# Weight loads of the state-space stage one tile sooner, the first blocks loaded in halves, the last blocks computed in column halves

## What is computed

```python
for i in range(DEPTH):
    hn = rmsnorm(h, g_mix[i])
    mix = mla_mixer(hn, ...) if i == 0 else s5_mixer(hn, ...)
    h = h + mix
    h = h + conv_ffn(rmsnorm(h, g_ffn[i]), ...)
return rmsnorm(h, g_final)
# s5_mixer
u = h @ w_in                                   # 64 groups of 16 channels
x_t = a * x_{t-1} + B u_t ; y = Re(C x) + D * u  # 64 complex states a group
y = gelu(y); val, gate = split(y @ w_glu); return val * sigmoid(gate)
```

## Time and profile before

| | |
|---|---|
| median of 3 runs | 1143.05 us (1139.31 to 1145.65) |
| the profiled execution's own time | 1146.58 us |
| its span in the profile | 1144.8 us |
| mean granted PE clock | 0.987 of full speed |

### The profile page before, as it was taken

How to read it: one execution, slowest core, us unless ns; L and a number is a source line. 1 busy time by engine, 2 the same in 40 slices (tenths; PEclk the granted TensorE clock), 3 DMA queues, 4 the chain that set the end, 5 groups by cost and what they waited for, 6 DMA issues and landing times.

```text
span 1144.8 us, 14849 instructions
## 1 busy us (share of the span) xinstructions
PE 1116.7 (98%) x5678; PEld 919.5 (80%) x5678; DVE 788.6 (69%) x1202; ACT 476.4 (42%) x721; POOL 57.9 (5%) x154
## 2 busy tenths in 40 slices
PE   8999899999999999999998999999999999999996
PEld 5787778888888888888887887888888888888885
DVE  6657857688787788978855885546765477635665
ACT  5556554455423543345451324334442244423442
POOL 3072004000000000000000000000000000000000
PEclk8999999999999999999998999999999999999998
DMA  6311103233343332433376663332333223232222
GB/s 210 102 59 52 37 20 111 78 114 126 106 130 111 116 123 92 148 111 120 89 260 202 175 186 93 94 109 75 109 95 108 93 92 95 90 111 92 93 78 87
DMA packets 62966, 125.68 MB, mean 110 GB/s; under 512 B 21808, under 2 KB 32560, under 8 KB 62896
## 3 DMA queue, kind: packets, MB, share of 16 engines
q1 hardware_dynamic: 61744, 120.54, 33.4%
q0 software_dynamic: 1152, 4.19, 1.1%
HBM read 110.04 MB, written 14.68 MB: 109 GB/s over the span
## 4 chain that ended last, share of the span: by engine, by line
PE 87%; DVE 5%; DMA 3%; DVEq 2%; ACT 1%; issue 1%; SPq 0%; ACTq 0%
PE bank L1507 27%; PE bank L1509 27%; PE bank L1508 27%; DVE MX L1057 1%; PE bank L1850 1%; DVE P L1065 1%; DVEq L1056 1%; PE bank L1799 1%; PE bank L1842 1%; DMA RAW<-in_w_wa 1%; ACT WH L505 1%; DMA RAW<-in_w_glu 1%; DVE WL L862 1%; DVE X L1289 1%; DMA ud_scratch<-UB 0%
## 5 line engine op out<-in xcount | busy, mean ns | idle before, releaser
L505 ACT ACTIVATE WH<-RAW 128x1024 fp32r<-128x1024 f32 (+1 forms) x184 | 190.0, 1034 | 392.2 <-PE bank L1509 352.6
L1507 PE MATMUL bank<-GH,WH 128*128 128x512 f32 x816 | 323.1, 396 | 3.2 <-DVE GL L920 3.2
L1508 PE MATMUL bank<-GL,WH 128*128 128x512 f32 x816 | 319.6, 392 | 0.0
L1509 PE MATMUL bank<-GH,WL 128*128 128x512 f32 x816 | 319.5, 392 | 0.0
L862 DVE TENSOR_TENSOR WL<-RAW,WH 128x1024 fp32r<-128x1024 f32 (+1 forms) x184 | 219.1, 1191 | 54.4 <-ACT WH L505 53.7
L1507 PE MATMUL bank<-AH,WH 128*128 128x512 f32 x596 | 235.2, 395 | 1.9 <-DVE WL L862 1.1
L1509 PE MATMUL bank<-AH,WL 128*128 128x512 f32 x596 | 232.2, 390 | 0.0
L1508 PE MATMUL bank<-AL,WH 128*128 128x512 f32 x596 | 232.0, 389 | 0.0
L1507 PEld LDWEIGHTS bank<-GH,WH 128*128 128x128 f32 x816 | 154.5, 189 | 36.7 <-DVE GL L920 4.1
L1509 PEld LDWEIGHTS bank<-GH,WL 128*128 128x128 f32 x816 | 154.5, 189 | 32.6
L1508 PEld LDWEIGHTS bank<-GL,WH 128*128 128x128 f32 x816 | 154.6, 189 | 32.4 <-issue 0.7
(11 more groups left out here) (270 smaller groups left out, 930.9 us busy)
## 6 DMA issues: line engine op xcount, KB each, us to landing
RAW<-in_w_up SPq DMA_DIRECT2D x88, 512.0 KB, 3.5
RAW<-in_w_dn SPq DMA_DIRECT2D x32, 512.0 KB, 3.5
RAW<-in_w_glu SPq DMA_DIRECT2D x16, 512.0 KB, 3.5
RAW<-in_w_dn SPq DMA_DIRECT2D x16, 384.0 KB, 3.0
RAW<-in_w_wo SPq DMA_DIRECT2D x8, 512.0 KB, 3.5
od_scratch<-OO SPq DMA_DIRECT2D x8, 512.0 KB, 3.7
kd_scratch<-KT SPq DMA_DIRECT2D x8, 512.0 KB, 4.9
O<-od_scratch POOLq DMA_DIRECT2D x8, 512.0 KB, 4.5
```

The costliest lines, as they stand in the source:

```text
L505: act_(WH[b % RH][:, :n], RAW[b % RW][:, :n], ACT.Copy).then_inc(s_hi, 1)
L1507: mm(out, wh, hi_[:, k, :], start=start, stop=False)
L1508: mm(out, wh, lo_[:, k, :], start=False, stop=False)
L1509: return mm(out, wl, hi_[:, k, :], start=False, stop=stop)
```

## The change

Three places are changed.

**Start.** Blocks 0 and 1 are loaded, split and consumed by halves of four units: first halves between the first x tiles, second halves behind x tile 3. One matmul of zeros fewer; PE takes two units of each block first, not three. Small tables go in another order, and on ACT and DVE blocks 2 and 3 are split between the squares at other points; the exponential of `ld` stands behind the squares.

**State-space stage.** In step t SP loads block win+5+t, where it loaded win+4+t, so each load stands one step ahead. TM4 and O2 of tile 4 come one step later. On DVE the low part of y tile 4 goes behind the states of the last tile.

**End.** The last three blocks are computed for columns 0 to 255 first, then for columns 256 to 511, with the sums, roots and spreading of the first half between the matmuls of the second. ACT multiplies tiles 0 to 6 by the gain beforehand, so DVE scales by the factor alone, in four instructions a half (3, 2, 2 and 1 tiles), each followed by its DMA.

```diff
-LAGS_AT = {1: 4, 3: 3, 4: 5, 6: 7}
+LAGS_AT = {2: 4, 3: 3, 4: 5, 6: 7}
...
+            def load_half(b, h):
+                sp.dma_start(RAW[b][:, HALF_W[h]], d["w_wa"][b][:, HALF_W[h]]).then_inc((s_rawh if h == 0 else s_raw)[b], 16)
...
+            load_half(0, 0)
+            x_in(0)
+            sp.dma_start(GAIN[:], d["gain"]).then_inc(s_par, 16)
+            x_in(1)
+            load_half(1, 0)
+            x_in(2)
+            x_in(3)
+            load_half(0, 1)
+            load_half(1, 1)
+            for k in range(4, KD):
+                x_in(k)
             load(2)
+            for n in ("lr", "li", "ld"):
+                sp.dma_start(small[n][:], d[n]).then_inc(s_sml, 16)
+            load(3)
...
                 if t >= 3:
                     y_out(t - 3)
-                if t >= 1:
-                    load(FIRST["win"] + 4 + t)
+                load(FIRST["win"] + 5 + t)
                 if t in LAGS_AT:
                     lags_in(LAGS_AT[t])
...
-            for k in range(4):
+            for k in range(2):
                 add_square("x", k, first=(k == 0))
             lo(2)
-            for k in range(4, KD):
+            for k in range(2, 6):
                 add_square("x", k)
             lo(3)
+            for k in range(6, KD):
+                add_square("x", k)
...
+            def final_squares(h):
+                for i, j in enumerate(LAST3):
+                    act.wait_ge(s_xh, 3 * h + i + 1)
...
+                    act_(SQ[j % 2][:, HALF[h]], X[:, j, HALF[h]], ACT.Square).then_inc(s_sqh, 1)
+                    if j < KD - 1:
+                        act_(X[:, j, HALF[h]], X[:, j, HALF[h]], ACT.Identity, scale=gain("final", j)).then_inc(s_xg, 1)
...
                     states(t - 2)
-                if t >= 4:
+                if t == NJ + 1:
+                    y_lo(t - 5)
+                if t >= 4 and t != NJ:
                     y_lo(t - 4)
...
+            final_add(KD - 1, 0)
             final_factor(0)
-            final_scale(0, range(0, 3))
+            final_add(KD - 3, 1)
+            final_scale(0, PARTS[:1])
+            final_sum(KD - 3, 1)
+            final_scale(0, PARTS[1:2])
+            final_add(KD - 2, 1)
...
-            pool.wait_ge(s_ur[1], 16)
+            pool.wait_ge(s_ur[2], 16)
             fetch(4)
...
-            for _ in range(5):
+            for _ in range(4):
                 mm(bank[3][:], ONES[:], WARM[:], start=True, stop=True)
...
+            def last_half(j, h, ks):
...
+                for k in ks:
+                    wh, wl = (w[b % RH][:, k * P:(k + 1) * P] for w in (WH, WL))
+                    out = bank[LAST[j, h]][:, HALF[h]]
+                    mm(out, wh, AH[:, k, HALF[h]], start=(k == 0), stop=False)
+                    mm(out, wh, AL[:, k, HALF[h]], start=False, stop=False)
+                    m = mm(out, wl, AH[:, k, HALF[h]], start=False, stop=(k == THIRDS[2][1] - 1))
...
+            for j in LAST3:
+                last_half(j, 0, range(6))
+            last_half(KD - 3, 1, range(4))
+            final_sums(0)
+            last_half(KD - 3, 1, range(4, 6))
+            last_half(KD - 2, 1, range(2))
+            final_spread(0)
+            last_half(KD - 2, 1, range(2, 6))
+            last_half(KD - 1, 1, range(6))
+            final_sums(1)
+            final_spread(1)
```

More of the change, by code:

```diff
@@ L698, in next_tile @@
                 square(X[:, j, :], SQ[j % 2], key, j)
+                if kind == "final":
+                    act_(X[:, j, :], X[:, j, :], ACT.Identity, scale=gain(kind, j)).then_inc(s_xg, 1)
             for j, b in enumerate(span("wo")):
@@ L850, in _ @@
             ffn(1, ("n_glu", "n_dn12", "final"))
-            final_std()
+            act_(STD[:], STD[:], ACT.Sqrt)
+            for h in range(2):
+                final_squares(h)
+                final_std(h)
         @block.vector
@@ L1258, in ffn @@
                     for j, b in enumerate(span(f"dn{l}{t}")):
+                        last = t == 2 and j == KD - 1
+                        if l == 1 and t == 2 and j in LAST3:
+                            continue
                         dve.wait_ge(s_mm, nth(b))
[L1260 to L1263 removed]
                         add_x(b, j)
@@ L1597, in spread @@
                 m.then_inc(s_sel, 1)
-            some(0, range(0, 3))
-            some(1, range(0, 3))
-            for k in range(3, KD):
+            some(0, range(0, 2))
+            some(1, range(0, 2))
+            for k in range(2, KD):
                 some(0, (k,))
@@ L1814, in ffn, with final_sums, final_spread @@
                             matrices(MAT_AT[b])
-                        whole(b, n, AH, AL)
+                        if b < NBLOCKS - 3:
+                            whole(b, n, AH, AL)
+            def last_half(j, h, ks):
+                b = NBLOCKS - KD + j
+                if 0 in ks and h == 0:
+                    ready(b)
+                for k in ks:
[4 more added lines that the diff above has]
+                    m = mm(out, wl, AH[:, k, HALF[h]], start=False, stop=(k == THIRDS[2][1] - 1))
+                if THIRDS[2][1] - 1 in ks:
+                    m.then_inc(s_lh, 1)
+            def final_sums(h):
+                pe.wait_ge(s_ssh, 2 * h + 2)
+                pe.wait_ge(s_sqh, 3 * h + 3)
+                for t in range(2):
+                    cols = slice((2 * h + t) * P, (2 * h + t + 1) * P)
+                    mm(bank[2 + 2 * h][:, t:t + 1], SS[:, cols], ONES[:, 0:1], start=True, stop=False)
+                    m = mm(bank[2 + 2 * h][:, t:t + 1], SQ[1][:, cols], ONES[:, 0:1], start=False, stop=True)
+                m.then_inc(s_mh, 1)
+            def final_spread(h):
+                pe.wait_ge(s_rch, h + 1)
+                for t in range(2 * h, 2 * h + 2):
+                    m = spread_column(bank[3 + 2 * h], t)
+                m.then_inc(s_bch, 1)
             ffn(0, "n_wo", TILE0["n_wo"])
```

160 lines of the change are left out of this document (86 added, 74 removed).

## The result

The changed kernel takes 1133.32 us (median of 5 runs, 1130.49 to 1135.14), the kernel before 1141.43 on the same chip (median of 5, 1139.31 to 1145.65). The ratio is 0.9921, with a 95% interval of 0.9904 to 0.9938: 9 us faster by the ratio (8.1 by the medians), where 14.2 were forecast. The median stands above the forecast's own range (1124.5 to 1132.5) and inside the wide one (1124 to 1135.5). The profiled execution took 1132.29 us.

A forecast was written before the change was run, and what follows sets the result against it. PE's queue of matmuls, busy 98% of the span, was taken as the bound. Start -6.0, state-space stage -7.5 and end -0.7 make -14.2, from 1143.05 to 1129 us; own range 1124.5 to 1132.5, wide range 1124 to 1135.5.

The forecast's parts named there:

- Start, -6.0: First 30 us: halved blocks bring PE's sums of x from 29.62 to 23.4; 6.0 us saved, bounds -2.5 to -7.0.
- the order of issue: Start: DMAs landing strictly as issued would bring old x tile 1 at about 5.9; the trace said 8.13.
- State-space stage, -7.5: Earlier load of win+5 shrinks PE's XI wait and keeps the clock up: 7.5 us saved, bounds -2.6 to -8.8.
- The delay of U, +1.0: State-space stage: the moved load collides with tile 0's read of U, making PE wait 1.0 us more (0 to 1.5).
- The other two waits for XI (0.8 us): State-space stage: PE's two shorter waits for XI have the same cause as the long one and go too, 0.8 us.
- The 3.89 us for the clock: State-space stage: low clock behind the long XI wait, 11.49 us against 7.60 to the next inputs; goes with the wait.
- End, -0.7: Last three blocks in column halves, half the scaling hidden: span ends 0.7 us sooner, bounds +1.5 to -2.5.
- outputs at 340 GB/s to the end: End: expected sign in the trace, the output DMAs running at that rate until the span ends.
- The start keeps a wait that costs the clock: Rival: x tile 1 and block 1 share the DMA rate; start gives only -2.5, total 1132.4; chance 0.15.
- rival of half-width matmuls bound by weight loads: End: 0.162 us per load sets the step, 108 matmuls take 17.5 us; end +4.5, total 1134.1; chance 0.06.
- rival of SP's queue: State-space stage: loads waiting on a later low part delay each of eight tiles; slower than before, 1149; chance 0.03.
- rival of a slow stretch that stays: State-space stage: tile 0's U comes later behind 0.5 MB of weights; stage only -2.6, total 1133.8; chance 0.10.

The follow-up runs named there:

- end alone: Only the edits of the end, on the kernel before: 1141.40 us (11 runs), ratio 0.9996.
- stage alone: Only the edits of the state-space stage, on the kernel before: 1134.33 us (5 runs), ratio 0.9919.
- without start: The whole change with its edits at the start undone: 1130.64 us (4 runs), ratio 0.9905.
- old start, states first: The whole change with its start undone and, on DVE, tile 0's states ahead of the low part of block win+5: 1130.32 us (6 runs), ratio 0.9908.
- one load: The kernel before with only the load of block win+5 moved, from step 1 to step 0: 1136.67 us (5 runs), ratio 0.9957.
- one load, low part last: The kernel before with block win+5 loaded in step 0 and y tile 4's low part behind the last tile's states: 1138.62 us (12 runs), ratio 0.9966.
- start alone: Only the edits of the start, on the kernel before: 1140.94 us (12 runs), ratio 0.9991.
- whole again: The changed kernel unedited, timed and traced a second time: 1132.30 us (4 runs), ratio 0.9907.
- whole third: The changed kernel unedited, timed and traced a third time: 1132.77 us (5 runs), ratio 0.9920.
- without end: The whole change with its edits at the end undone: 1134.36 us (6 runs), ratio 0.9929.
- states first: The whole change with, on DVE, tile 0's states ahead of the low part of block win+5: 1130.72 us (4 runs), ratio 0.9900.

## Why the prediction was right in its range and wrong in its terms

All 13 traces, cut at four marks of PE's timeline: the sums of x; from the first KH,QH matmul of attention to the inputs of tile 0 (between these two marks lie 71.2 or 71.3 us in every trace); from there to the XR matmuls of the last tile; from there to the end of the span.

| trace | start | sums of x | attention to inputs | stage | rest |
|---|---|---|---|---|---|
| before | old | 29.62 | 503.58 | 81.88 | 458.46 |
| end alone | old | 26.39 | 501.93 | 82.96 | 457.20 |
| stage alone | old | 24.59 | 503.22 | 75.15 | 458.32 |
| without start | old | 24.37 | 501.90 | 73.27 | 457.21 |
| old start, states first | old | 24.49 | 501.87 | 72.84 | 457.46 |
| one load | old | 24.46 | 501.91 | 77.71 | 458.26 |
| one load, low part last | old | 24.28 | 502.00 | 75.71 | 458.38 |
| start alone | new | 22.51 | 503.49 | 82.07 | 458.72 |
| after | new | 22.67 | 502.47 | 76.56 | 457.48 |
| whole again | new | 23.22 | 503.41 | 76.73 | 458.02 |
| whole third | new | 23.25 | 503.67 | 73.27 | 457.99 |
| without end | new | 23.39 | 503.70 | 77.17 | 458.71 |
| states first | new | 23.09 | 504.06 | 72.83 | 457.51 |

**Start, -6.0: mis-sized, the term that failed.** The new start was forecast well: the sums at 23.4, measured 23.02 as the mean of six. Wrong was what it was held against. The step took x tile 1 at 8.13 and block 1 at 9.94 as the kernel's own and gave the reason that "later transfers took part of the rate"; then it counted the 2.32 us wait and 15 matmuls at the low clock as what the change could take away. Six other traces of the same instructions have the sums at 24.28 to 26.39; in five of them the clock from 10 to 20 us is 1.00 although PE waits up to 1.47 us for GL. The 8.13 that the prediction held against the order of issue was that run's own as well: in the other six ACT takes x tile 1 at 6.1 to 6.54, where that order gave 5.9. Over seven old and six new traces the start gives 25.46 - 23.02 = 2.4 us. And 1.1 of it is gone before the first inputs (502.34 on average with the old start, 503.47 with the new). Part of that is systematic: PE's last wait for P in attention is 0.91 or 0.92 us in all seven traces with the old start and 1.26 or 1.27 in all six with the new, behind a gap on DVE that nothing in the profile explains. PE and DVE of after:

```profile
141.59 0.55 PE L1787 MATMUL bank<-IDENT,P 128*128 128x128 f32 x3 [1.27 <-DVE P L1108]
```

```profile
140.27 0.69 DVE L1100 TENSOR_REDUCE MX<-bank 128x1 f32<-128x512 f32 x1 [0.42 <-issue]
```

The rest is a drop of the clock between 100 and 130 us, in five of six new traces and two of seven old ones. The whole third and the old start with the states first, same stretch:

```profile
105.00:110.00 5.00, 5.00 (x22) 3.73 (x21) 3.22 (x14) 2.70 (x10) 0.00 (x0) 0.70 0.02 5
```

```profile
105.00:110.00 5.00, 4.52 (x26) 3.73 (x27) 4.21 (x16) 3.78 (x12) 0.00 (x0) 1.00 0.02 5
```

Both had just waited 1.61 us for P at the same matmul. Whether the new start makes this drop likelier, or seven and six traces fell so, was not settled. Net the start is worth 1.3 us by the traces, and only 0.4 without the trace of before (24.76 and 502.14 on the old side); timed alone 0.8 (up to 2.6, or nothing), and in the whole it did not show at all. Why x tile 1 and block 1 landed so late in the one trace is open.

**State-space stage, -7.5: right in size, by two errors of opposite sign.** The stage's mean is 82.30 in the three traces with the old loads and 75.36 in the six with the new ones: -6.9. By its steps: the landing of 4.8 us was exact, and XI came 0.51 us late instead of 0.3. The delay of U, +1.0, was not there: PE waits 0.25 us for the first U (0.38 before), and from its read to its inputs pass 3.03 us with the load right behind (3.15 before), so 0.5 MB issued 0.4 us later took nothing from it. (The sum also takes off the 0.3 us that, by the prediction's own words, the 1.0 would hide.) The other two waits for XI (0.8 us) went, but not with the one load, as the two runs with one load show; the edits behind them were undervalued, since without them half of the gain is missing. The 3.89 us for the clock is the step that went wrong in this trace: "with it goes what cost the clock". In the six traces the step still takes 9.4 us on average, so 1.8 of the 3.9 us stayed, and the 1.0 that U did not cost made up for half of them. Wait at the first XR matmuls, and time from there to the next inputs, in all traces:

| wait, us | to the next inputs, us |
|---|---|
| 0, 0 (states first, both) | 7.60, 7.59 |
| 0.30, 0.34, 0.37 | 7.60, 7.59, 7.60 |
| 0.51, 0.51 | 10.76, 9.21 |
| 0.65, 0.66, 1.10 | 10.78, 9.18, 10.76 |
| 4.12, 4.21, 4.60 | 11.49, 11.69, 11.68 |

Waits of the forecast's size (0.30 to 0.37) kept the clock in three traces; the 0.2 to 0.8 us more of four of the six traces with the changed stage cost 1.6 to 3.2. Which side of this the unchanged kernel fell on was chance: its three traces have 0.37, 0.51 and 0.65. `states_first` shows the cause at this place by taking the wait away and changing nothing else. The two traces at 9.2 (stage alone, one load) have the old start and those at 10.8 the new; why is open.

The Trainium skill, page "TensorE: Matmul & The Clock Gate", section "What's actually happening", has the clock set by how busy the engine has been recently. The rows do not contradict that; what they add is that the length of a wait alone does not tell it: 0.51 us was enough at the first XR matmuls of this stage, while 1.49 us at the XR matmuls one tile later and 1.47 us at the start were not.

**End, -0.7: right in size.** The rest of the program takes 458.48 us on average in six traces with the old end and 457.55 in seven with the new: -0.9. The 14.7 us from the first of the three blocks to the last unit were 14.4, the step 0.12, the chain to the scaling 3.4 (forecast 3.5), and from the start of the scaling to the end of the span 5.85 us (forecast 5.6 to the last landing and 0.4 more): 0.95 for the first piece of three tiles (forecast 1.0) and 4.9 behind it (forecast 5.0). The sign "outputs at 340 GB/s to the end" did not come: the DMAs are idle at 1125.

**Sum.** -1.3, -6.9 and -0.9 make -9.1, and the three timings of the whole say -9.0, -10.6 and -9.1 (1 minus the ratio, times 1141.6). That they meet so closely is partly luck: without the trace of before in the means the sum is -0.4 - 7.2 - 0.9 = -8.5. Of the 5.1 us by which -14.2 overshot, 4.7 are the start's. The time of 1129 was missed by less, 4.3 us, because its base, the median 1143.05 of three runs, was itself 1.3 us or more above later medians of the same kernel (1141.43 to 1141.76). The forecast's range, "the bounds roughly half each", should have reached 1134 on the slow side (half of 3.5 + 4.9 + 2.2 us), where the result lies; it was put at 1132.5. "The start keeps a wait that costs the clock" was the nearest rival in size (-2.5), but by another way: the new start keeps none, the old one mostly had none. The rival of half-width matmuls bound by weight loads is out (0.12 us a step); its price of +4.5 was also 0.5 too high, since 17.5 us stand against the 12.8 that the -0.7 already holds. The rival of SP's queue is out too: the stage is shorter, and PE waits for no XI behind tile 0. The rival of a slow stretch that stays was right in what one sees (10.76 and 10.78 us in two traces of the whole), but U did not make it: the 0.51 us for XI did.

## What to carry to other kernels

Before a wait at the start of a program is counted as gain, look at it in a second trace: what hangs on the landing of the first DMAs moved by 2 us from run to run here, while the waits of attention that hang on the order of instructions (1.61, 1.74, 1.51 us) stayed within 0.02. A profiled run 5 us above or below the median of its kernel is not the typical one; both happened here. And where a wait costs the clock, shrinking it may not be enough: take it away with margin, here by letting the states go first.

## What the runs showed of the hardware

- At one place of the program, the first XR matmuls, PE waits of 0 to 0.37 us left the clock at 1.00 and waits of 0.51 us and more were followed by a stretch at 0.50, in 13 traces without an exception. At the same instructions one tile later 1.49 us left it up, and at the start 1.47 us.
- The same DMAs at the start of the program, in the same order, brought block 1 to ACT at 7.51 to 9.94 us and x tile 1 at about 6.1 to 8.13 (seven traces).
- 0.5 MB of weights issued 0.4 us behind a small read did not delay that read measurably: from its issue to its use 2.78 to 3.03 us in the ten traces with the load there, 2.78 to 3.15 in the three without.
- An added 0.42 us gap on DVE at 140 us, with no releaser in the profile, appeared in PE's wait of every trace whose start was changed, 120 us after the change. The kernel before has such gaps at other places (0.45 us at 316.39, 0.43 at 554.28). What makes them is open.
